# Down projection of a decoder layer: weights streamed in 512 columns past stationary activations, output with tokens on partitions

## The reference

```python
h = rmsnorm(x, norm_ffn_g[l])
x = x + jnp.square(jax.nn.relu(h @ w_up[l])) @ w_down[l]
return rmsnorm(x, final_g)
```

## Time and profile before

| | us |
|---|---|
| median of 3 runs | 1580.27 (1580.24 to 1581.42) |
| span of the profiled execution | 1578.5 |
| PE busy | 1550.8 (98%) |
| DVE busy | 1127.0 (71%) |
| ACT busy | 752.3 (48%) |
| DMA, share of 16 engines | 56.8%, 182 GB/s |

### The profile page before, as it was taken

The page is one execution under the profiler, slowest core; times in us unless marked ns, Lnnn a source line. Parts: engine busy times, 40 slices in busy tenths (PEclk is TensorE's granted clock), DMA queues, the critical chain, the costliest instruction groups (busy, mean ns, idle before and its releaser), DMA issues.

```text
span 1578.5 us, 25519 instructions
## 1 busy us (share of the span) xinstructions
PE 1550.8 (98%) x8875; PEld 1348.0 (85%) x8875; DVE 1127.0 (71%) x1461; ACT 752.3 (48%) x938; POOL 22.6 (1%) x27
## 2 busy tenths in 40 slices
PE   5999999999999999999999999999999999999997
PEld 5888888888888888888888888888888888888886
DVE  7657888989999988666667665566655665566664
ACT  4444444466664556455445443344434443344443
POOL 5000000000000000000000000000000000000000
PEclk8999999999999999999999999999999999999998
DMA  5665565655445555555555565556555655555552
GB/s 173 193 195 179 178 193 182 205 161 160 159 159 185 188 184 190 186 182 196 182 194 179 184 193 190 180 180 191 192 182 178 193 179 194 187 185 178 195 177 103
DMA packets 285698, 286.58 MB, mean 182 GB/s; under 512 B 9005, under 2 KB 284085, under 8 KB 285652
## 3 DMA queue, kind: packets, MB, share of 16 engines
q1 hardware_dynamic: 285652, 285.98, 56.8%
HBM read 283.32 MB, written 2.10 MB: 181 GB/s over the span
## 4 chain that ended last, share of the span: by engine, by line
PE 97%; DVE 2%; ACT 0%; DMA 0%; issue 0%; ACTq 0%; SPq 0%; DVEq 0%
PE acc L985 59%; PE acc L984 30%; PE acc L981 4%; PE acc L982 2%; DVE h_hl L595 1%; PE acc L989 1%; PE acc L1038 0%; DVE h_hl L591 0%; DVE w_lo L584 0%; DMA x_tok<-in_x 0%; PE acc L1061 0%; PE acc L1060 0%; PE acc L1059 0%; PE acc L994 0%; DVE res L852 0%
## 5 line engine op out<-in xcount | busy, mean ns | idle before, releaser
L985 PE MATMUL acc<-h_hl,w_hi 128*128 128x512 f32 x2460 | 871.6, 398 | 0.0
L580 DVE TENSOR_TENSOR w_lo<-w_raw,w_hi 128x1024 fp32r<-128x1024 f32 x533 | 642.4, 1221 | 237.1 <-ACT w_hi L408 231.7
L408 ACT ACTIVATE w_hi<-w_raw 128x1024 fp32r<-128x1024 f32 x533 | 554.9, 1055 | 451.2 <-PE acc L985 445.5
L984 PE MATMUL acc<-h_hl,w_lo 128*128 128x256 f32 x2460 | 692.2, 281 | 5.8 <-DVE w_lo L584 5.8
L985 PEld LDWEIGHTS acc<-h_hl,w_hi 128*128 128x128 f32 x2460 | 463.8, 189 | 108.4
L984 PEld LDWEIGHTS acc<-h_hl,w_lo 128*128 128x128 f32 x2460 | 466.1, 189 | 11.3 <-issue 5.2
L985 PE MATMUL acc<-m_hl,w_hi 128*128 128x512 f32 x1200 | 424.5, 397 | 0.0
L984 PE MATMUL acc<-m_hl,w_lo 128*128 128x256 f32 x1200 | 337.2, 281 | 0.0
L985 PEld LDWEIGHTS acc<-m_hl,w_hi 128*128 128x128 f32 x1200 | 225.4, 188 | 52.9
L984 PEld LDWEIGHTS acc<-m_hl,w_lo 128*128 128x128 f32 x1200 | 226.6, 189 | 1.7
L510 ACT ACTIVATE second<-acc 128x512 f32<-128x512 f32 x106 | 63.4, 598 | 161.9 <-PE acc L985 161.8
(11 more groups left out here) (156 smaller groups left out, 843.3 us busy)
## 6 DMA issues: line engine op xcount, KB each, us to landing
w_raw<-in_w_in SPq DMA_DIRECT2D x200, 512.0 KB, 3.5
w_raw<-in_w_up SPq DMA_DIRECT2D x128, 512.0 KB, 3.7
w_raw<-in_w_down SPq DMA_DIRECT2D x128, 512.0 KB, 3.3
w_raw<-in_w_mix_out SPq DMA_DIRECT2D x32, 512.0 KB, 4.3
w_raw<-in_w_sconv_out SPq DMA_DIRECT2D x16, 512.0 KB, 3.3
w_raw<-in_w_attn_out SPq DMA_DIRECT2D x16, 512.0 KB, 3.2
w_raw<-in_w_conf_out SPq DMA_DIRECT2D x16, 512.0 KB, 4.1
x_tok<-in_x SPq DMA_DIRECT2D x4, 512.0 KB, 7.6
```

The costliest lines, as they stand in the source:

```text
L408: act.activation(w_hi[:, ahead % RING], w_raw[:, ahead % RING], ACT.Copy).then_inc(hi_done, 1)
L580: dve.tensor_tensor(w_lo[:, q], w_raw[:, q], w_hi[:, q].bitcast(F32), ALU.subtract).then_inc(lo_done, 1)
L984: pe.matmul(*narrow, start=False, stop=False)
L985: last = pe.matmul(*wide, start=False, stop=final)
```

## The change

Only `down` and the end are changed. In `down` a slab is now 256 rows x 512 columns, still 512 KB and 1024 elements per partition, so that ACT's and DVE's work on it has the same size. The stationary operand is a 128x128 block of activations (128 hidden channels x 128 tokens, hi or lo), the moving one is 512 columns of `w_hi` or `w_lo`. For each of a slab's two row tiles and each half of the tokens there are three matmuls of 512 columns, into one PSUM bank, where before there were 8 wide and 8 narrow ones: 12 per slab. A group is 8 slabs for 512 output channels, a chunk has 4 groups.

The output has tokens on partitions. So the residual is turned around once: in trip 0 of `up` in chunk 0, PE transposes `res` four tiles a slab (`transpose_res`, 8 times) and ACT copies each result to `y_tok`. DVE adds a group's two banks to `y_tok`. In chunk 3 the gain, now a row `gf_row` of 2048 on every partition (1 MB, one DMA in `up`'s first trip), is multiplied in by DVE, and ACT squares with a sum along the free dimension. The transposes of chunk 3 and the final sum over partitions are gone.

```diff
+DCOLS = 512
+DKT = KT * COLS // DCOLS
+DROWS = DKT * P
+KDOWN = D // DROWS
+NBLK = D // DCOLS
...
-    for name in ("up", "down"):
-        ph = phases[name] = Phase(name, 4, [KFULL] * 2, s, g)
+    for name, trips, groups in (("up", 4, [KFULL] * 2), ("down", NBLK // 2, [KDOWN] * 2)):
+        ph = phases[name] = Phase(name, trips, groups, s, g)
...
-    loop("down")
+    body(PH["down"], 0, 0)
+    loop("down", first=1)
...
+                if ph.name == "down":
+                    sp.dma_start(wide_rows(w_raw[:, k % RING]), w[bass.ds(row, DROWS), bass.ds(col, DCOLS)]
+                                 .rearrange("(a p) n -> p a n", p=P)).then_inc(raw_full[k % RING], 16)
...
+                        sp.wait_ge(evac_done, PH["mix"].group0)
+                        rows(gf_row[:, :], final_g[None, :].to_broadcast((P, D)), gf_in)
...
+                            act.wait_ge(y_t, k + 1)
+                            act.activation(y_tok[:, :, 2 * k * P:(2 * k + 2) * P],
+                                           aux[k % 2][:, :].rearrange("p (b n) -> p b n", b=2), ACT.Copy).then_inc(y_copied, 1)
...
+                        for b in range(2):
+                            if j or b:
+                                act.wait_ge(y_sq, 2 * j + b)
+                            act.activation(square[:, :], y_tok[:, b, j * DCOLS:(j + 1) * DCOLS], ACT.Square,
+                                           accum_out=part_sq[:, b, j:j + 1]).then_inc(y_sq, 1)
...
-                        r = res[:, bass.ds(j * 2, 2), :]
-                        add_total(r)
+                        for b, done in ((0, half_sum), (1, evac_done)):
+                            dve.tensor_tensor(y_tok[:, b, cols], acc[:, bank(ph, n) + b, :], y_tok[:, b, cols],
+                                              ALU.add).then_inc(done, 1)
...
+                                dve.tensor_tensor(yg_tok[:, b, cols], y_tok[:, b, cols], gf_row[:, cols],
+                                                  ALU.mult).then_inc(y_gain, 1)
...
+                for a in range(DKT):
+                    kt = i * DKT + a
+                    first, final = kt == 0, kt == size * DKT - 1
+                    for m in range(2):
+                        h_h, h_l = (m_hl[:, kt, h, m * P:(m + 1) * P] for h in range(2))
+                        pe.matmul(acc[:, b + m, :], h_h, hi[:, a, :], start=first, stop=False)
+                        pe.matmul(acc[:, b + m, :], h_h, lo[:, a, :], start=False, stop=False)
+                        last = pe.matmul(acc[:, b + m, :], h_l, hi[:, a, :], start=False, stop=final)
...
-                        pe.wait_ge(hid_lo, c * 8 + 2 * (i + 1))
+                        pe.wait_ge(hid_lo, c * 8 + (i + 1))
+                        products_down(ph, c, t, k)
```

More of the change, by code:

```diff
@@ L97 @@
 CHUNKS = FF // D
-CHUNK_SLABS = 2 * 4 * PH["up"].nslabs
-CHUNK_GROUPS = 2 * 4 * PH["up"].ngroups
+CHUNK_SLABS = sum(PH[name].trips * PH[name].nslabs for name in ("up", "down"))
+CHUNK_GROUPS = sum(PH[name].trips * PH[name].ngroups for name in ("up", "down"))
 TOTAL = PH["up"].slab0 + CHUNKS * CHUNK_SLABS
@@ L200, in build @@
         y_tok = view("y_tok", merged, 0, [P, 2, D])
+        yg_tok = view("yg_tok", res, 0, [P, 2, D])
+        gf_row = view("gf_row", z_ba, 0, [P, D])
+        square = view("square", z_ba, D, [P, DCOLS])
         q_t = sb("q_t", [P, HT, SEQ])
@@ L269, in both, with wide_rows @@
             return t2[:, None, :].to_broadcast((P, 2, SEQ))
+        def wide_rows(slab):
+            return slab.rearrange("p (k b) n -> p k (b n)", k=DKT)
         def bank(ph, n):
@@ L548, in trip @@
                         j = 2 * t + n
+                        act.wait_ge(half_sum, g + 1)
                         act.wait_ge(evac_done, g + 1)
[L550 to L558, removed]
+                        for b in range(2):
[3 more added lines that the diff above has]
+                                           accum_out=part_sq[:, b, j:j + 1]).then_inc(y_sq, 1)
             walk(act, trip)
@@ L986, in products, with products_down @@
                 last.then_inc(slab_used, 1)
+            def products_down(ph, c, t, k):
+                n, i, size = ph.slabs[k]
+                s, g, q = slab_of(ph, c, t, k), group_of(ph, c, t, n), k % RING
+                pe.wait_ge(lo_done, s + 1)
+                if i == 0:
+                    pe.wait_ge(evac_done, g - 1)
+                b = bank(ph, n)
+                hi, lo = wide_rows(w_hi[:, q]), wide_rows(w_lo[:, q])
+                for a in range(DKT):
[6 more added lines that the diff above has]
+                        last = pe.matmul(acc[:, b + m, :], h_l, hi[:, a, :], start=False, stop=final)
+                last.then_inc(slab_used, 1)
             def transposed(dst, src):
@@ L1128, in transpose_y @@
                         last = transposed(aux[j % 2][:, b * 2 * P + e * P:b * 2 * P + (e + 1) * P],
-                                          pair[j % 2][:, e, b * P:(b + 1) * P])
+                                          res[:, 2 * j + e, b * P:(b + 1) * P])
                 last.then_inc(y_t, 1)
             walk(pe, trip)
-            transpose_y(7)
-            pe.wait_ge(fold3, 1)
-            for b in range(2):
-                last = pe.matmul(aux[2][:, b:b + 1], stat[:, b * P:(b + 1) * P], ones[:, 0:1], start=True, stop=True)
-            last.then_inc(stat3, 1)
 _INS = ["x", "norm_mix_g", "w_in", "gate_b", "conf_dw", "conf_ln_g", "conf_ln_b", "w_conf_out", "sconv_w",
```

83 lines of the change are left out of this document (36 added, 47 removed).

## The result

| | before | after |
|---|---|---|
| median of 4 runs, us | 1580.54 (1580.24 to 1581.42) | 1567.27 (1566.47 to 1568.13) |
| ratio | | 0.9916, interval 0.9903 to 0.9928 |
| span of the profiled execution, us | 1578.5 | 1564.7 |

The forecast was 1575.1 in a range of 1568 to 1586. The changed kernel run again beside other kernels gave 1567.78 and a ratio of 0.9911 (0.9895 to 0.9928).

A forecast was written before the change was run, and what follows sets the result against it. The prediction took PE, busy 98% of the span, to bound the kernel through its matmuls' spacing and number. Its terms, -4.1 - 0.2 - 3.1 + 3.5 - 1.3 = -5.2 us, gave 1575.1 us, range 1568 to 1586.

The forecast's parts named there:

- The matmuls: In `down`, 12 matmuls a slab at 0.2315 us, 2.778 instead of 2.821: 4.1 us less in looped chunks, 0.2 in chunk 3.
- the fast rhythm: In written-out chunk 3, a pair of one wide and one narrow matmul takes 0.3475 us.
- a cost for each matmul: Rival: loss above streaming is fixed per matmul (0.0163 us), a wide one in `down` takes 0.2296; 1572.1 us, chance 0.17.
- the slow rhythm: In the loops, three quarters of `up` and `down`, a pair of one wide and one narrow matmul takes 0.353 us.
- The Trainium skill's rule: Matmul starts N/2.4 + 2.5 ns apart, saving 1.3 us in all; kept as a rival at 1578.1 us, chance 0.08.
- Transposes: Chunk 3 loses seven rounds of 0.44 us (3.1 less); `up`'s first trip gains eight (3.5 more).
- ACT and DVE in that trip: In `up`'s first trip, eight added ACT copies make rstd up to 1.8 us later, covered by 3.3 us slack: no cost.
- The gain's DMA: 1 MB more on SP's queue in `up`, 2.7 us against 5.0 us of load slack: no cost.
- Down's loads with longer rows: `down` slabs loaded in rows of 2 KB instead of 1 KB can only land sooner, and landing has slack.
- The tail: From the last add to the scaling, some 2.6 us instead of 3.90: 1.3 us less, bounds 1.0 to 1.5.
- The slower rival: In `down`, streaming from the weight ring that ACT and DVE write costs 0.24 us a matmul: 1588.1 us, chance 0.15.
- the slow-rhythm rival: Loss goes by columns, `down` runs at 0.2350 us a matmul throughout: +0.1 us, so 1580.4, chance 0.22.

The follow-up runs named there:

- the run of halves: Changed kernel with every 512-column product in `down`, except a group's first, cut into two of 256 columns: 1586.23 us, span 1584.4.
- the run on one constant operand: Changed kernel whose `down` matmuls all read one constant float32r tile, the down projection left out: span 1563.9 us.
- two and two: Two wide matmuls, then two narrow: in the changed kernel's products except `down`'s, 1558.28 us; in all products of the kernel before, 1568.76 us.

## Why the prediction was wrong, point by point

**What bounds.** Right. PE is nearly the whole chain before and after, and no engine or DMA became late.

**The matmuls.** Here it failed, in the term 12 x 0.2315 = 2.778. It measures 12 x 0.2267 = 2.720, and the 0.058 between them, over 128 slabs, are 7.4 of the 8.3 us by which the sum was off; the rest is 0.5 in the transposes and 0.3 in the tail. The value was taken from two wide matmuls that meet at a boundary amid alternation, and from the columns' share of the fast rhythm. Both were measured in a mixture, and the traces show that a wide matmul among narrow ones takes 0.231 to 0.236 on average, by the rhythm, and steadily 0.2267 only among its like. The alternative, a cost for each matmul, was among the rivals with 0.17 and was right in kind. Two things went wrong in weighing it. Its size was taken from the slow rhythm (0.0163), which gave 1572.1; from the fast one it is (0.3475 - 0.320) / 2 = 0.0137, a matmul 0.2270, a slab 2.724, and the sum -9.3 - 1.6 - 0.4 - 0.9 = -12.2 us. And the narrow one's 0.12, which is 0.1067 + 0.0133, was held against it because it was less than half of a slow pair's loss. It is what a stream of narrow ones takes (0.120 in the run of halves), so it was evidence for the rival; in the mixture itself the narrow ones take 0.112 to 0.121, and that this one stood at 0.12 is chance. The rhythm on top should have been taken away before the rest was shared out.

**The order of wide and narrow** was not seen as a cost at all. The forecast tied the slow rhythm to loops, and put "three quarters" of `up` and `down` in it; it was seven eighths, and a written-out part was slow and a looped one fast, as shown above. "No wait in the trace says why" was the place at which to ask whether `down`, without alternation, could be in the slow rhythm; in all runs whose `down` has only full wide float32r matmuls and full loads it was not. Of the 0.101 a slab that the looped chunks won, 4 x 0.0133 = 0.053 are the four matmuls saved and the other 0.048 is the slow rhythm left behind. All loads were issued, also the second one of the same block (8359 loads for 8359 matmuls on the page), so that condition of the forecast held.

**The Trainium skill's rule.** The trace of before had 353 ns for a pair against 325, and to set the 1.3 us by that rule aside was right: the four matmuls saved a slab brought 128 x 0.053 = 6.8 us. In the Trainium skill, "TensorE: Matmul & The Clock Gate", section "Back-to-back issue gap", the formula is that of an isolated matmul, with nothing for a weight load. The bfloat16 stream here shows its 2.5 ns with a load for each matmul, the float32r stream 13.3.

**Transposes.** 3.1 right, 3.5 measured 3.0, since 0.3 us of PE's wait for the sum over partitions covered a part, which the sum had not used. One of the eight rounds in the chain:

```profile
856.95 0.44 PE acc L1018 x4
```

**ACT and DVE in that trip.** Right. The reciprocal starts at 850.22, 1.4 us later than in the earlier trace rows, and rstd is read at 855.16, 3.2 us after its end:

```profile
850.22 1.75 DVE L816 RECIPROCAL rstd<-rstd 128x256 f32<-128x256 f32 x1 [0.99 <-ACT rstd L567]
...
855.16 0.69 DVE L868 TENSOR_TENSOR pair<-pair,rstd 128x512 f32<-128x512 f32 x1
```

**The gain's DMA.** Right in its cost, nothing, and wrong in its length. The 2.7 us were reckoned from the highest rate in the rows. From issue to landing it took 7.7, where `up`'s loads of half the size take 3.8 by the median; by that difference it held the queue for some 3.9 us, an estimate that is still within the slack of 5.0:

```profile
gf_row<-in_final_g SPq DMA_DIRECT2D x1, 1024.0 KB, 7.7
```

It was issued at 836.1 us. Between 838 and 870 us no engine waits for a DMA, and in the whole trace none waits for a load of `up` or `down`; all that ACT's split waits for there is PE:

```profile
ACT w_hi L428 <- PE acc L995: 4.5, 5, 1.8
```

**Down's loads with longer rows** "can only land sooner": wrong, without a price. They land later, 4.7 us after their issue by the median where it was 3.3. Rows of 2 KB are not shown to be the cause: with the same loads the other runs with the changed `down` have medians of 3.6 to 4.8, and the lowest two, 3.6 and 3.7, are the two whose `down` takes longest for a slab (2.79 and 2.88 us). The row of the page before, then of after:

```profile
w_raw<-in_w_down SPq DMA_DIRECT2D x128, 512.0 KB, 3.3
```

```profile
w_raw<-in_w_down SPq DMA_DIRECT2D x128, 512.0 KB, 4.7
```

The slack of 5.0 us was reckoned with 4.0; with 4.7 and a ring's turn of 10.9 it is still some 3.9, and no wait shows.

**The tail.** 1.3 forecast, with bounds of 1.0 to 1.5; 1.6 measured. The reduction and the handovers were smaller than allowed for.

**The slower rival** fell with 0.2267 in `down`, and its mechanism with the run on one constant operand: reading the ring costs nothing that shows. Its turning point was misreckoned: the parts of the sum cancel at 0.2349 a matmul, not at 0.2355, as the slow-rhythm rival (0.2350, +0.1 us) says too.

## What to carry to other kernels

Where TensorE is the bound, count matmuls as well as columns: each float32r one, with its load, cost 0.0133 us beside its columns here, so the same columns in 512s and not in 256s are some 5% cheaper (2 x 0.120 against 0.2267). Look at the starts of the matmuls, by pattern, before pricing anything from them: a loss made of two causes, here a fixed cost and a rhythm, has to be split first, and a value taken from a mixture does not hold for a pure stream. If wide and narrow matmuls must alternate, try two and two: here this order alone was worth 12.6 us of 1581.

## What the runs showed that was not expected

- The same two matmuls in the same order take 0.3467 or 0.353 a pair, for hundreds of microseconds at a time. Loops, the operand and the place of the wide one do not decide it by themselves, and the same code of `up` ran in both. What decides is open; I know only that two and two, in two kernels, never showed the slow one.
- After narrow ones, about five wide matmuls take 0.228 to 0.236 before they settle at 0.227.
- Halving the weight load's columns, and the output partitions with them, made the stream slower, 0.230 for 0.2267.
- bfloat16 tiles: 0.216 for 512 columns, a cost of 0.0025 against float32r's 0.0133.
- 512 KB in rows of 2 KB landed 1.4 us later than in rows of 1 KB by the medians of the two traces, 0.3 to 1.5 later over all runs. No run looked into the cause.
